# Feature-wise A projections, ScalarE's normalisation and an in-place relu in a two-layer hybrid decoder trunk

## The chip, the cores and the metric

The kernel runs on one core of one Trainium2 chip. Its time is the device time of one execution in microseconds (us). Before the change three runs took 775.15, 771.83 and 767.22 us, a median of 771.83; the profiled execution took 768.9 us.

The core's engines work beside each other, each through its own instructions in order, and wait for each other by semaphores: TensorE (PE, with its weight loads as PEld), VectorE (DVE), ScalarE (ACT), GpSimd (POOL), and SyncE (SP), which issues the DMAs.

## The reference

A trunk of two layers over 512 tokens of width 1024. Each layer normalises the state, multiplies it by one wide matrix `w_in` (its columns belong to four attention branches of four heads each), and brings the gated branches back through `w_out`:

```python
proj = rms_norm(h, norm_pre[layer]) @ w_in[layer]
y_a = mla_branch(a_cq, a_ckv, a_kr, ...) * silu(a_g)      # A: low-rank q and kv, rotary key
y_b = dilated_branch(b_q, b_k, b_v, bias_b) * silu(b_g)   # B
y_c = sparse_branch(c_q, ..., bias_c, k_top) * silu(c_g)  # C: an indexer picks 128 keys
y_d = diff_branch(d_q, d_k, d_v, ...) * silu(d_g)         # D: two softmax maps
h = h + rms_norm(concat(y_a, y_b, y_c, y_d) @ w_out[layer], norm_post[layer])
```

The parts that the change touches:

```python
# A
q = (rms_norm(c_q, q_norm) @ w_uq)       # 192 -> 4 heads x (64 plain + 32 rotary)
kv = (rms_norm(c_kv, kv_norm) @ w_ukv)   # 128 -> 4 heads x (64 key + 64 value)
apply_rope(x) = concat([x1*cos - x2*sin, x1*sin + x2*cos])   # on q's 32 and one shared 32-wide key
p = softmax(mask(q_nope @ k_nope.T + q_rope @ k_rope.T) * 96**-0.5);  o = p @ v
# C's indexer, 8 heads of 32
score = einsum('bqhs,bqh->bqs', relu(q_idx @ k_idx.T), w_idx)   # then mask and top 128
```

## The kernel before, in words

Everything is fp32. Products that need the precision are split into a high and a low part, each in a faster fp32r form, and made of three products (`three`, L1215 to L1217): ScalarE copies the high part (L733 for weights), GpSimd subtracts to get the low part of the weights (`low`, L694), VectorE the low part of activations.

One list, `SEQUENCE`, sets the order of the work; each engine walks through it and issues its share of each step. Steps are: `unit`, one projection of 128 features by 512 tokens or 128 tokens by 256 features (24 matmuls, in one of two PSUM work banks, emptied by ScalarE and VectorE); `idx`, one head of the indexer (three matmuls into three PSUM score banks); `topk`, rounds of VectorE's maximum search; and for each of 16 jobs (a head of D, B, C, A in this order: jobs 0 to 3 are D, 4 to 7 B, 8 to 11 C, 12 to 15 A) `scores`, `norm`, `turn` and `pv`. `layer_steps` lays them out so that while job j makes its scores, job j-1 is normalised and turned and job j-2 or a pair of jobs is multiplied with its values.

For a job with one softmax map: TensorE writes a block of scores; VectorE adds the bias and takes the maximum (L1070, reading PSUM); ScalarE takes the exponential with its sum (L837); VectorE inverts the sums (L981) and scales the four blocks of probabilities, 128, 256, 384 and 512 wide (L984, in `normalise`); TensorE turns them (L1321); ScalarE copies them out of PSUM (L850); TensorE multiplies them with the values (L1349, two jobs at a time). D's jobs have two maps, which VectorE joins (L977).

`TURN_LATE` names the jobs (6, 7, 9, 10, 12) in whose slot the last two turned blocks of the previous job are put off to the next slot, behind the first scores and the `norm` there. Where two jobs are multiplied next, TensorE then waits for just these two copies.

The indexer: ScalarE takes the relu from the score bank into one of four SBUF buffers (L828), VectorE adds the weighted rows into `select` (L1042). TensorE may refill a score bank once the relu is done.

A's projections before are token-wise: per block of 128 tokens (`aup`) one product gives q (L1382, L1383), one k and v (L1386); VectorE scales and rotates q (L1142 to L1151), ScalarE scales k and v (L870 to L874), and `aturn` turns eight 128 x 96 blocks (L1397), which ScalarE copies to `aqk` (L882). They stand in the slots of jobs 10 and 11.

```python
             10: [("aup", 0), ("aup", 1), ("aturn", 0)],
             11: [("aup", 2), ("aturn", 1), ("aup", 3), ("aturn", 2), ("aturn", 3)]}
```

In the slots of jobs 12 to 15 no projections are left beside the attention jobs; from job 16's slot on the output projection begins (`ya`).

## Time and profile before

| | us |
|---|---|
| three runs | 775.15, 771.83, 767.22 |
| profiled execution, whole | 768.9 |
| its span | 767.0 |
| busy in the span: PE / DVE / ACT / POOL | 690.5 / 450.4 / 328.7 / 218.4 |

The profile is of one execution. A busy PE is not a PE at its peak: its matmuls overlap and their ends are modelled, so what a matmul costs is read from the starts of two that follow each other. The granted clock is TensorE's, as a share of 2.4 GHz; 0.50 is its lower level, 1.2 GHz. The chain of waits that the page shows for the end covers only the last 0.2% of the span, so it doesn't help here; the waits of TensorE and its timeline do.

### The profile page before, as it was taken

How to read it: one execution, taken by the hardware profiler on the slowest of the kernel's cores; microseconds unless marked ns; L12 is line 12 of the kernel's file. 1: busy time of each engine (PE TensorE's matmuls, PEld its weight loads, DVE VectorE, ACT ScalarE, POOL GpSimd, SP SyncE). 2: the span in 40 equal slices, each digit the busy share in tenths (PEclk: the TensorE clock that was granted, in tenths of full speed). 3: DMA queues.
4: the chain of work that ended last, by engine and by line, in shares of the span. 5: the costliest groups of instructions: out<-in, count | busy, mean ns of one | idle time of the engine just before them, and what ended most of it. 6: DMA issues, size and time to landing. Idle time of an engine off the chain costs nothing. (4 is left out here: it accounts for less than half of the span.)

```text
span 767.0 us, 10353 instructions
## 1 busy us (share of the span) xinstructions
PE 690.5 (90%) x3836; PEld 553.9 (72%) x3836; DVE 450.4 (59%) x1067; ACT 328.7 (43%) x750; POOL 218.4 (28%) x91
## 2 busy tenths in 40 slices
PE   3996999998989899889998999999898989988996
PEld 2885877787776674448997887788787767444896
DVE  4211597987688645561182158888978864556214
ACT  4422534654223445571434345456432344457221
POOL 1332241424035430200335342324323543020020
PEclk9998999997899976999999999999999997699999
DMA  8457963423122110202353487542322221020112
GB/s 259 123 188 233 258 185 111 124 76 106 55 69 69 69 56 1 109 1 80 96 157 111 129 254 228 157 138 69 98 70 68 70 70 56 0 108 3 43 42 110
DMA packets 66753, 81.47 MB, mean 106 GB/s; under 512 B 10720, under 2 KB 52320, under 8 KB 66703
## 3 DMA queue, kind: packets, MB, share of 16 engines
q1 hardware_dynamic: 66703, 80.81, 34.2%
q8 instruction: 31, 0.51, 0.3%
q14 instruction: 19, 0.16, 0.1%
HBM read 70.28 MB, written 13.93 MB: 110 GB/s over the span
## 5 line engine op out<-in xcount | busy, mean ns | idle before, releaser
L694 POOL TENSOR_TENSOR w_low<-w_raw,w_high 128x2048 fp32r<-128x2048 f32 (+2 forms) x39 | 175.8, 4507 | 435.3 <-ACT w_high L733 435.3
L1215 PE MATMUL bank<-uT,w_high 128*128 128x512 f32 x400 | 161.2, 403 | 0.0
L1217 PE MATMUL bank<-uT,w_low 128*128 128x512 f32 x400 | 159.2, 398 | 0.0
L1216 PE MATMUL bank<-uT,w_high 128*128 128x512 f32 x400 | 159.1, 398 | 0.0
L837 ACT ACTIVATE probs<-probs,negmax 128x128 f32<-128x128 f32 (+3 forms) x160 | 89.1, 560 | 99.6 <-DVE negmax L1070 99.0
L1215 PEld LDWEIGHTS bank<-uT,w_high 128*128 128x128 f32 x400 | 76.2, 190 | 18.7 <-issue 1.9
L1217 PEld LDWEIGHTS bank<-uT,w_low 128*128 128x128 f32 x400 | 76.2, 190 | 18.0
L1216 PEld LDWEIGHTS bank<-uT,w_high 128*128 128x128 f32 x400 | 76.3, 191 | 16.5
L733 ACT ACTIVATE w_high<-w_raw 128x2048 fp32r<-128x2048 f32 (+2 forms) x40 | 74.7, 1868 | 29.8 <-DMA w_raw<-in_w_out 23.7
L1215 PE MATMUL bank<-w_high,mix 128*128 128x256 f32 x256 | 72.4, 283 | 1.0 <-DVE mix L1155 1.0
L1216 PE MATMUL bank<-w_low,mix 128*128 128x256 f32 x256 | 71.6, 280 | 0.0
L1217 PE MATMUL bank<-w_high,mix 128*128 128x256 f32 x256 | 71.6, 280 | 0.0
L1321 PE MATMUL bank<-ident,probs 128*128 128x128 f32 x320 | 52.3, 294 | 20.0 <-DVE probs L984 7.7
L1215 PE MATMUL bank<-w_high,uT 128*128 128x256 f32 (+1 forms) x192 | 55.9, 291 | 12.6 <-ACT values L800 6.0
L1321 PEld LDWEIGHTS bank<-ident,probs 128*128 128x128 f32 x320 | 38.3, 149 | 38.0 <-DVE probs L984 11.9
L850 ACT ACTIVATE turned<-bank 128x512 f32<-128x512 f32 (+3 forms) x128 | 48.5, 430 | 20.3 <-PE bank L1321 19.4
L963 DVE MAX8 best<-select 128x8 f32<-128x512 f32 (+2 forms) x96 | 53.6, 558 | 1.9
L1216 PE MATMUL bank<-w_low,uT 128*128 128x256 f32 (+1 forms) x192 | 54.7, 285 | 0.0
L1217 PE MATMUL bank<-w_high,uT 128*128 128x256 f32 (+1 forms) x192 | 54.6, 284 | 0.0
L964 DVE MATCH_REPLACE8 select<-best,select 128x512 f32<-128x512 f32 (+2 forms) x96 | 52.1, 543 | 0.0
L984 DVE TENSOR_SCALAR probs<-probs,inv 128x128 f32<-128x128 f32 (+1 forms) x96 | 49.7, 581 | 0.8
L1215 PEld LDWEIGHTS bank<-w_high,mix 128*128 128x128 f32 x256 | 48.2, 188 | 1.8 <-DVE mix L1155 1.4
(145 smaller groups left out, 1119.0 us busy)
## 6 DMA issues: line engine op xcount, KB each, us to landing
w_raw<-in_w_in SPq DMA_DIRECT2D x28, 1024.0 KB, 5.4
w_raw<-in_w_out SPq DMA_DIRECT2D x8, 1024.0 KB, 4.9
parts_dram<-staging SPq DMA_DIRECT2D x12, 512.0 KB, 5.9
strips<-strips_dram SPq DMA_DIRECT2D x24, 256.0 KB, 4.6
dqk<-parts_dram SPq DMA_DIRECT2D x24, 256.0 KB, 4.3
hX<-in_x SPq DMA_DIRECT2D x8, 512.0 KB, 5.8
strips_dram<-table_dram SPq DMA_DIRECT2D x1, 3328.0 KB
qidx<-parts_dram SPq DMA_DIRECT2D x12, 256.0 KB, 4.2
```

What stands on the lines that cost most here:

```text
L694: nc.gpsimd.tensor_tensor(w_low[:, s, :, 0:w], w_raw[:, s, :, 0:w], w_high[:, s, :, 0:w].bitcast(F32), ALU.subtract).then_inc(w_low_done, 1)
L733: nc.scalar.activation(w_high[:, g % SLOTS, :, 0:w], w_raw[:, g % SLOTS, :, 0:w], ACT.Copy).then_inc(w_high_done, 1)
L837: nc.scalar.activation(pr, pr, ACT.Exp, bias=negmax[:, j % 4, m, q:q + 1], scale=-1.0, accum_out=sums[:, j % 4, m, q:q + 1]).then_inc(exp_ ...
L850: nc.scalar.activation(turned[j % 2][:, TOFF[kb]:TOFF[kb] + w], bank[:, TURN + t % 2, 0:w], ACT.Copy).then_inc(turn_emptied, 1)
L963: after(nc.vector.max(best[:], row))
L964: after(nc.vector.match_replace(row, best[:], row, MARK))
L984: ins = nc.vector.tensor_scalar(probs[bufs[0]][:, sl], probs[bufs[0]][:, sl], inv[:, i, 0, q:q + 1], None, ALU.mult)
L1215: nc.tensor.matmul(out_ap, lh, rh, start=start, stop=False)
L1216: nc.tensor.matmul(out_ap, lh, rl, start=False, stop=False)
L1217: return nc.tensor.matmul(out_ap, ll, rh, start=False, stop=stop)
L1321: ins = nc.tensor.transpose(bank[:, TURN + t % 2, (q - kb) * P:(q - kb + 1) * P], buf[:, POFF[q] + kb * P:POFF[q] + (kb + 1) * P], ident[:])
```

## The change

Three edits.

**The indexer's relu.** ScalarE writes it back into the score bank, and VectorE's weighted sum reads it there. TensorE may refill the bank only once that sum is done.

**The normalisation.** For jobs of B, C and A (4 to 15) VectorE only inverts the sums; ScalarE scales the four blocks, in place, at the same step of the list. D's jobs stay as they are.

**A's projections.** They are made feature-wise: `aq` per head (128 features, the 32 rotary ones twice, the second time with their halves swapped, by 512 tokens), `ak` for two heads of keys, `av` for two blocks of values. There is no scaling by token at the copies: k's root is brought into `latkv` by one product of the roots with the identity and one VectorE multiply (`aroot`), q's root goes in as the scale of A's bias step. q's rotation is one multiply with a table (`trig`), since the score product over 128 rows adds the two halves. The shared key is rotated by GpSimd and copied to all heads by DMA. The eight turned blocks fall away. The q weights come in six DMAs for two and k and v's in two for one, and six small DMAs per layer are new for the tables and the rotary key.

```diff
-             10: [("aup", 0), ("aup", 1), ("aturn", 0)],
-             11: [("aup", 2), ("aturn", 1), ("aup", 3), ("aturn", 2), ("aturn", 3)]}
+             10: [("aq", 0), ("aq", 1), ("aroot",), ("aq", 2)],
+             11: [("aq", 3), ("ak", 0), ("ak", 1), ("av", 0), ("av", 1)]}
...
# SyncE
                 if step == ("norm", 3):
-                    sp.dma_start(wuq[:, 0, :], mla_w_uq[l, 0:P, :]).then_inc(a_loaded, 16)
...
+                    sp.wait_ge(scores_ready, l * NS + NS_IDX)
+                    sp.dma_start(trig[HD:P, :], rope).then_inc(trig_loaded, 16)
+                if step == ("norm", 8):
+
+                    sp.wait_ge(bias_ready, (l + 1) * HEADS)
+                    wait_unit_emptied(sp, l * NU + UNIT_AT[("unit", "cq", 1)])
+                    sp.dma_start(trig2[HD:A_QK, :], rope[A_ROPE:2 * A_ROPE, :]).then_inc(krx_loaded, 16)
+                    sp.dma_start(krx[HD:HD + 16, :], latq[HD + 16:A_QK, 1, :]).then_inc(krx_loaded, 16)
+                    sp.dma_start(krx[HD + 16:A_QK, :], latq[HD:HD + 16, 1, :]).then_inc(krx_loaded, 16)
+                if step == ("norm", 9):
+
+                    sp.wait_ge(kr_ready, l + 1)
+                    sp.wait_ge(scores_ready, l * NS + NS_IDX + S_AT[8])
+                    for first in (HD, A_QK):
+                        sp.dma_start(aqk[first:first + A_ROPE, 1, :, :],
+                                     latq[HD:A_QK, 1, :].unsqueeze(1).to_broadcast([A_ROPE, HEADS, SEQ])
+                                     ).then_inc(krope_loaded, 16)
...
# GpSimd
+                if step == ("norm", 8):
+
+                    pool.wait_ge(trig_loaded, 16 * (l + 1))
+                    pool.wait_ge(krx_loaded, 48 * (l + 1))
...
+                    nc.gpsimd.tensor_tensor(raw, raw, trig[HD:A_QK, :], ALU.mult).then_inc(kr_step, 1)
+                    pool.wait_ge(kr_step, 2 * l + 1)
+                    nc.gpsimd.tensor_tensor(turn, turn, trig2[HD:A_QK, :], ALU.mult).then_inc(kr_step, 1)
+                    pool.wait_ge(kr_step, 2 * (l + 1))
+                    nc.gpsimd.tensor_tensor(raw, raw, turn, ALU.add).then_inc(kr_ready, 1)
...
# ScalarE
                         act.wait_ge(scores_ready, n + 1)
-                        if relus[0] >= 4:
-                            act.wait_ge(index_added, relus[0] - 3)
-                        nc.scalar.activation(probs[relus[0] % 4][:, 0:WID[q]],
-                                             bank[:, SCORE + n % 3, 0:WID[q]], ACT.Relu).then_inc(relu_done, 1)
-                        relus[0] += 1
+                        b = bank[:, SCORE + n % 3, 0:WID[q]]
+                        nc.scalar.activation(b, b, ACT.Relu).then_inc(relu_done, 1)
...
+                if kind == "norm" and MAPS[step[1]] == 1:
+                    j = step[1]
+                    buf = probs[probs_buffers(j)[0]]
+                    act.wait_ge(inv_ready, scaled(l, j))
+                    for q in range(NB):
+                        pr = buf[:, POFF[q]:POFF[q] + WID[q]]
+                        ins = nc.scalar.activation(pr, pr, ACT.Copy, scale=inv[:, j % 4, 0, q:q + 1])
+                    ins.then_inc(probs_scaled, 1)
...
+                if kind == "aq":
+                    n = l * NU + UNIT_AT[step]
+                    act.wait_ge(unit_ready, n + 1)
+                    nc.scalar.activation(aqk[0:HD, 0, step[1], :], bank[0:HD, unit_bank(n), :], ACT.Copy
+                                         ).then_inc(high_written, 1)
...
# VectorE
-                    after(nc.vector.reciprocal(inv[:, i, 0], sums[:, i, 0]))
-                    for q in range(NB):
-                        sl = slice(POFF[q], POFF[q] + WID[q])
-                        ins = nc.vector.tensor_scalar(probs[bufs[0]][:, sl], probs[bufs[0]][:, sl],
-                                                      inv[:, i, 0, q:q + 1], None, ALU.mult)
-                ins.then_inc(probs_ready, 1)
+                    nc.vector.reciprocal(inv[:, i, 0], sums[:, i, 0]).then_inc(inv_ready, 1)
...
-                        nc.vector.scalar_tensor_tensor(row, probs[relus[0] % 4][:, 0:WID[q]], wi[:, q, h:h + 1],
+                        n = l * NS + h * 3 + SEL_BLOCKS.index(q)
+                        nc.vector.scalar_tensor_tensor(row, bank[:, SCORE + n % 3, 0:WID[q]], wi[:, q, h:h + 1],
                                                        before, ALU.mult, ALU.add).then_inc(index_added, 1)
...
+                        scale = negroot[:, q:q + 1] if br == "A" else -1.0
...
+                if kind == "aq":
...
+                    nc.vector.tensor_tensor(aqk[HD:P, 0, step[1], :], bank[HD:P, unit_bank(n), :], trig[HD:P, :],
+                                            ALU.mult).then_inc(emptied_by["dve"], 1)
...
# TensorE
                     if ii < NS_IDX:
-                        pe.wait_ge(relu_done, ll * NS_IDX + ii + 1)
+                        pe.wait_ge(index_added, ll * NS_IDX + ii + 1)
...
+                    nc.tensor.matmul(b, wuq[:, 0, h, :], latq[:, 0, :], start=True, stop=False)
+                    nc.tensor.matmul(b, wuq[0:QL - P, 1, h, :], latq[0:QL - P, 1, :], start=False, stop=True
+                                     ).then_inc(unit_ready, 1)
...
+                        ins = nc.tensor.matmul(b[:, tb * P:(tb + 1) * P],
+                                               roots[:, r, NB + tb:NB + tb + 1].to_broadcast([P, P]), ident[:],
+                                               start=True, stop=True)
...
+                    nc.tensor.matmul(b, wukv[:, 0, step[1] * P:(step[1] + 1) * P], latkv[:], start=True, stop=True
+                                     ).then_inc(unit_ready, 1)
...
+                        ins = nc.tensor.matmul(b[:, half * 256:(half + 1) * 256], latkv[:, tb * P:(tb + 1) * P],
+                                               wukv[:, 1, :], start=True, stop=True)
```

How the order moves, at three places of the first layer. The names in the rows: `values_61` holds the values of the branch at work, `probs_55` to `probs_58` are the four probability buffers, `turned_59` and `turned_60` the two for turned blocks, `bank` is PSUM.

ScalarE at the third block of B's values (slot of job 6), before:

```order
L837 ACTIVATE probs_57,sums<-probs_57,negmax 128x128 [waits shifted]
L837 ACTIVATE probs_57,sums<-probs_57,negmax 128x256 [waits shifted]
L800 ACTIVATE values_61<-bank 128x256 [waits unit_ready,pv_ready] x3
L733 ACTIVATE w_high<-w_raw 128x8x256 [waits w_loaded0]
L850 ACTIVATE turned_60<-bank 128x512 [waits turn_ready,pv_ready]
```

and with the change:

```order
L874 ACTIVATE probs_57,sums<-probs_57,negmax 128x128 [waits shifted]
L874 ACTIVATE probs_57,sums<-probs_57,negmax 128x256 [waits shifted]
L882 ACTIVATE probs_56<-probs_56,inv 128x128 [waits inv_ready]
L882 ACTIVATE probs_56<-probs_56,inv 128x256
L882 ACTIVATE probs_56<-probs_56,inv 128x384
L882 ACTIVATE probs_56<-probs_56,inv 128x512
L840 ACTIVATE values_61<-bank 128x256 [waits unit_ready,pv_ready] x3
L773 ACTIVATE w_high<-w_raw 128x8x256 [waits w_loaded0]
```

The four scalings of job 5 stand between the exponentials of job 6 and the copies of B's values.

TensorE in the slot of job 10, before (the first rows of A's projections, then the turn of job 9):

```order
L1382 MATMUL bank<-wuq,latq 128x384 [waits emptied_by_dve,a_folded]
L1383 MATMUL bank<-wuq,latq 128x384
L1386 MATMUL bank<-wukv,latkv 128x512 [waits emptied_by_dve]
L1382 MATMUL bank<-wuq,latq 128x384 [waits emptied_by_dve,a_folded]
L1383 MATMUL bank<-wuq,latq 128x384
L1386 MATMUL bank<-wukv,latkv 128x512 [waits emptied_by_act]
L1321 MATMUL bank<-ident,probs_56 128x128 [waits turn_emptied,probs_ready]
L1321 MATMUL bank<-ident,probs_56 128x128 x3
```

and with the change:

```order
L1405 MATMUL bank<-latq,wuq 128x512 [waits emptied_by_dve,a_folded]
L1406 MATMUL bank<-latq,wuq 128x512
L1405 MATMUL bank<-latq,wuq 128x512 [waits emptied_by_dve,a_folded]
L1406 MATMUL bank<-latq,wuq 128x512
L1351 MATMUL bank<-ident,probs_56 128x128 [waits turn_emptied,probs_scaled]
L1351 MATMUL bank<-ident,probs_56 128x128 x3
```

Four products of 512 columns stand where two groups of 384, 384 and 512 columns stood; `ak` and `av` come in the next slot, and the products with `tokq` and `tokk` are gone.

ScalarE in the slot of job 13, before:

```order
L850 ACTIVATE turned_60<-bank 128x512 [waits turn_ready,pv_ready]
L850 ACTIVATE turned_60<-bank 128x384 [waits turn_ready]
L837 ACTIVATE probs_56,sums<-probs_56,negmax 128x128 [waits shifted]
L837 ACTIVATE probs_56,sums<-probs_56,negmax 128x256 [waits shifted]
L850 ACTIVATE turned_60<-bank 128x256 [waits turn_ready]
L850 ACTIVATE turned_60<-bank 128x128 [waits turn_ready]
L837 ACTIVATE probs_56,sums<-probs_56,negmax 128x384 [waits shifted]
L837 ACTIVATE probs_56,sums<-probs_56,negmax 128x512 [waits shifted]
```

and with the change:

```order
L895 ACTIVATE turned_60<-bank 128x512 [waits turn_ready,pv_ready]
L895 ACTIVATE turned_60<-bank 128x384 [waits turn_ready]
L874 ACTIVATE probs_56,sums<-probs_56,negmax 128x128 [waits shifted]
L874 ACTIVATE probs_56,sums<-probs_56,negmax 128x256 [waits shifted]
L882 ACTIVATE probs_55<-probs_55,inv 128x128 [waits inv_ready]
L882 ACTIVATE probs_55<-probs_55,inv 128x256
L882 ACTIVATE probs_55<-probs_55,inv 128x384
L882 ACTIVATE probs_55<-probs_55,inv 128x512
L895 ACTIVATE turned_60<-bank 128x256 [waits turn_ready]
L895 ACTIVATE turned_60<-bank 128x128 [waits turn_ready]
L874 ACTIVATE probs_56,sums<-probs_56,negmax 128x384 [waits shifted]
L874 ACTIVATE probs_56,sums<-probs_56,negmax 128x512 [waits shifted]
```

The scaling of job 12 stands ahead of the last two copies of job 11's turned blocks, on which the product of jobs 10 and 11 waits.

## Rows read from the trace of the kernel before

**Rows 1.** The page, its first part: busy us, share of the span, instructions

```profile
PE 690.5 (90%) x3836; PEld 553.9 (72%) x3836; DVE 450.4 (59%) x1067; ACT 328.7 (43%) x750; POOL 218.4 (28%) x91
```

**Rows 2.** Waits of TensorE: in total, times, longest us

```profile
PE bank L1321 <- DVE probs L984: 7.7, 6, 2.8
```

**Rows 3.** Windows, columns: length, PE, PEld, DVE, ACT, POOL, clock, DMA share, GB/s

```profile
184.00:197.00 13.00, 13.00 (x47) 10.82 (x46) 8.72 (x24) 3.91 (x8) 4.54 (x1) 0.50 0.08 22
223.00:231.00 8.00, 5.00 (x40) 4.65 (x39) 7.59 (x28) 2.90 (x8) 1.60 (x1) 1.00 0.00 0
264.00:273.00 9.00, 9.00 (x38) 5.22 (x38) 4.57 (x14) 5.38 (x15) 2.92 (x3) 0.62 0.01 3
283.00:299.00 16.00, 16.00 (x41) 9.15 (x41) 9.93 (x32) 4.01 (x14) 4.61 (x2) 0.50 0.01 2
321.00:347.00 26.00, 21.35 (x114) 12.36 (x115) 18.66 (x64) 18.60 (x55) 0.00 (x0) 1.00 0.14 52
552.00:562.00 10.00, 8.62 (x56) 7.32 (x57) 8.72 (x21) 4.79 (x10) 2.49 (x2) 1.00 0.09 28
...
629.00:637.00 8.00, 8.00 (x32) 4.61 (x32) 4.38 (x14) 5.38 (x15) 2.92 (x3) 0.62 0.01 3
```

**Rows 4.** TensorE by time near job 7's wait: start, us, what, idle

```profile
263.95 0.98 PE L1321 MATMUL bank<-ident,probs 128*128 128x128 f32 x7 [2.80 <-DVE probs L984]
...
273.11 0.50 PE L1215 MATMUL bank<-uT,w_high 128*128 128x512 f32 x1
```

**Rows 5.** VectorE's normalisation at the same place, and at its shortest

```profile
256.74 7.16 DVE L984 TENSOR_SCALAR probs<-probs,inv 128x128 f32<-128x128 f32 x4
...
322.91 1.27 DVE L984 TENSOR_SCALAR probs<-probs,inv 128x128 f32<-128x128 f32 x4
```

**Rows 6.** GpSimd by time at the same place

```profile
258.68 4.60 POOL L694 TENSOR_TENSOR w_low<-w_raw,w_high 128x2048 fp32r<-128x2048 f32 x1
```

**Rows 7.** Groups of instructions on ScalarE: busy us, mean ns of one, idle before

```profile
L837 ACT ACTIVATE probs<-probs,negmax 128x128 f32<-128x128 f32 (+3 forms) x160 | 89.1, 560 | 99.6 <-DVE negmax L1070 99.0
...
L870 ACT ACTIVATE tokk<-bank,roots 128x256 f32<-128x256 f32 x8 | 3.8, 476 | 24.1 <-PE bank L1386 24.1
```

**Rows 8.** VectorE's groups by form: the weighted sum, a reader of PSUM

```profile
L1042 DVE SCALAR_TENSOR_TENSOR select<-probs,wi,select 128x512 f32<-128x512 f32 x14 | 26.2, 1875 | 12.1 <-ACT probs L828 12.1
...
L1070 DVE CUSTOM_DVE_ANT_0 probs<-bank,strips 128x512 f32<-128x512 f32 x24 | 16.5, 689 | 1.0 <-PE bank L1298 0.6 <-PE bank L1217 0.2
```

**Rows 9.** TensorE by time at the indexer's last head

```profile
100.34 0.51 PE L1279 MATMUL bank<-kidx,qidx 96*128 96x512 f32 x1 [0.71 <-ACT probs L828]
```

**Rows 10.** TensorE and ScalarE by time at the third block of B's values

```profile
226.48 0.36 PE L1215 MATMUL bank<-w_high,uT 128*128 128x256 f32 x1 [3.00 <-ACT values L800]
225.97 0.63 ACT L800 ACTIVATE values<-bank 128x256 f32<-128x256 f32 x2
```

**Rows 11.** TensorE, ScalarE at the products of jobs 4, 5 and 8, 9

```profile
243.75 2.37 PE L1349 MATMUL bank<-turned,values 128*64 128x512 f32 x16 [1.71 <-ACT turned L850]
305.28 2.38 PE L1349 MATMUL bank<-turned,values 128*64 128x512 f32 x16 [1.54 <-ACT turned L850]
304.70 0.53 ACT L850 ACTIVATE turned<-bank 128x256 f32<-128x256 f32 x2
```

**Rows 12.** TensorE by time in A's projections

```profile
307.58 0.91 PE L1382 MATMUL bank<-wuq,latq 128*128 128x384 f32 x2
...
309.26 1.12 PE L1386 MATMUL bank<-wukv,latkv 128*128 128x512 f32 x2
310.23 0.60 PE L1397 MATMUL bank<-ident,tokq 128*96 128x128 f32 x4
...
319.26 0.61 PE L1397 MATMUL bank<-ident,tokq 128*96 128x128 f32 x4 [1.20 <-ACT aqk L882]
```

**Rows 13.** TensorE by time: first score of A, first turn of its last head

```profile
321.04 2.58 PE L1301 MATMUL bank<-aqk 96*128 96x128 f32 x8 [0.36 <-ACT aqk L882]
347.32 0.93 PE L1321 MATMUL bank<-ident,probs 128*128 128x128 f32 x7
```

211 lines of the change are left out of this document (97 added, 114 removed).

## The prediction

> **What bounds the kernel now.** I read the page's busy times first: TensorE is busy 90% of the span, VectorE much less [rows 1]. So work taken off VectorE pays only where TensorE waits for it. Next the waits of TensorE: the reader is to see that L984, the normalisation, is in them with 7.7 us, 2.8 the longest [rows 2]. Third the windows: in them the reader is to see that TensorE's clock falls to its lower level, 1.2 GHz, in the same places of both layers: after job 7's wait, and after the one-column products ahead of A's projections [rows 3]. A fall costs half of its length. The places are where the change acts, so I go through one layer by place; the second repeats it nearly to the microsecond. About 1% (7.7 us) is what this kernel's measurement can tell from no change. The sum is made against the profiled execution, 768.9 us; the median of the three runs, 771.8, lies 2.9 above it.
>
> **The normalisation's price.** On VectorE four scalings take 1.27 us undisturbed and 7.16 at job 7, where GpSimd's additions and a 4.60 us `w_low` run beside them [rows 5, 6]. On ScalarE the row does not exist. Above it lies the exponential over the same four widths, mean 560 ns, so 2.24 us for four; below, VectorE's 1.27. A scaling by a pointer, 256 wide, takes 476 ns [rows 7] against the exponential's 560 at mean 320. Back-to-back instructions overlap by about 0.1 us. I take 1.85 us, 24 times in the run, 44 us of ScalarE's time.
>
> **Job 7 (gain).** TensorE waits 2.80 us for L984, then runs turns, C's scores and the product of jobs 6 and 7 until 273.11 [rows 4]; the window from 264 to 273 has a mean clock of 0.62, in layer two 629 to 637 likewise [rows 3]. From the end of the wait's unit at 261.15 (263.95 less 2.80) that is 11.96 us. With ScalarE doing it, GpSimd does not matter and the scaling is done 2 us before TensorE wants it: the wait goes, and some 7.4 us at half clock become 3.7. Late next are the copies of job 7's last two turned blocks, behind job 8's exponentials: about 1.1 us. Net -5.4 us.
>
> **B's values, job 6 (loss).** TensorE waits 3.00 us for ScalarE's first copy of B's values, which starts at 225.97 right behind job 6's first two exponentials [rows 10]. In the changed order job 5's four scalings stand between. The wait grows by 1.85 to 4.85. The cause of the first 3.00, VectorE's late scores, stays.
>
> **Products of jobs 4, 5 and 8, 9 (loss).** Both wait for the last two copies of turned blocks, 1.71 and 1.54 us [rows 11], and both times a scaling now stands ahead of these copies: +1.85 and +1.8.
>
> **A's projections (gain).** One token block costs TensorE 1.68 us for q (307.58 to 309.26) and 0.97 for k and v; four turned blocks have records of 0.60 that overlap [rows 12], and I take 0.48. Before: four times 2.65, eight times 0.48, and 0.5 for the rotary key, 14.9 us. After, at the row's price of 0.97 for 512 fp32 columns: eight products for q 7.8, `ak` 1.9, `av` 2.0 (four of 256), `aroot` 1.1 (four of 128), 12.8. That is -2.1 at full clock. About 5.6 us of the old work stands in the 283 to 299 window at 0.50 [rows 3] and 3.9 of the new, which saves 1.7 more; `aroot` gives back 0.5: -1.2. The waits for tokk, tokq and aqk go, the largest 1.20 [rows 12], 2.3 in all. New are two small waits, for the last of the q banks and at A's first score: +0.6. Net -5.0 us.
> I cost the rotary key at nothing. Its chain is a load, three GpSimd additions over 512, each a quarter of a `w_low`'s 4.60 [rows 6], so 3.5 us, and a copy to all heads. It can start when the last `fill` is done, soon after job 7's turn at 263.95, and must end by A's first score at 321.04 [rows 4, 13]: even with 10 us for each of two DMA steps it ends 30 us early. Without that cover it would cost its length, up to 24. The six DMAs more in SyncE's queue hold nothing up: the weight load behind them waits for the gate's unit anyway.
>
> **A's jobs (loss).** From 321 to 347 no projection covers TensorE. ScalarE is busy 18.6 of 26 us there [rows 3]; five normalisations (jobs 11 to 15) add 9.25, which makes 27.9. So ScalarE now sets the pace. Walking its order from A's first score at 321.04 to the first turn of job 15, at 347.32 before [rows 13], which leaves 1.4 us of ScalarE waiting for scores, I get 29.3 us for 26.3: +3.0 (ends: 1.6, the pure fill, and 9.25, if every scaling lands on the path; the order has other work of TensorE beside most).
>
> **The indexer.** VectorE's weighted sum over 512 has a mean of 1.88 us, disturbed by GpSimd; a reader of PSUM of this width takes 0.69 undisturbed [rows 8]. That frees some 8 us of VectorE per layer, which nobody on the path waits for: VectorE catches up with TensorE in the stretch of D's jobs anyway. But a score bank is free only after relu and sum. Behind the first heads a projection stands between and hides this; the last two heads stand together, where TensorE waits 0.71 now [rows 9], and each bank comes up to 0.69 later, the sum's own length [rows 8]: +0.6 (ends: -1.2 if the end of the contention counts most, +3 if each head loses 0.4).
> The Trainium skill ("ScalarE: Activation LUTs", section "Step-by-step: what each stage is for") says that ScalarE writes PSUM faster than SBUF, which would make the in-place relu cheaper than before. No row here shows such a write. By that rule the three relus of a head would end sooner, and the term would be nearer 0, the sum 1 us lower.
>
> **The sum.** Per layer: job 7 -5.4, B's values +1.85, jobs 4 and 5 +1.85, jobs 8 and 9 +1.8, A's projections -5.0, A's jobs +3.0, the indexer +0.6: -1.3, or -2.6 for two.
> The clock is left. A wait does not make it fall for certain: the same stretch of the program has 0.50 in layer one (184 to 197) and 1.00 in layer two (552 to 562) [rows 3]. Three waits of 3.4 to 4.9 us are new or longer, and one of 2.8 is gone. I take one fall more than before in one of the layers, +3.7 by job 7's price. 768.9 - 2.6 + 3.7 = 770; against the median **773 us**.
>
> **The rivals.**
> *Forecast, the stalls trade (0.38):* 773, own range 765 to 781.
> *Slower, the clock falls at the new waits (0.31).* Place: B's values (4.85 us), the products of jobs 4, 5 (3.56) and 8, 9 (3.35). For it: the 2.80 wait does it in both layers. Against it: the 3.00 wait does not (223 to 231 at 1.00), nor do A's waits (321 to 347) [rows 3]. Price 3.7 each; after jobs 8, 9 come A's fp32 products, which stayed at 0.50 for the 16 us of 283 to 299, so up to 8 there. It decides from two falls on: 773 + 7.4 = 780; all of them in both layers would give 800. Its middle is 787. The Trainium skill ("TensorE: Matmul & The Clock Gate", section "HAM oscillation — how this bites in real kernels") describes the mechanism, a wait that makes the engine start again at the low clock.
> *Faster, ScalarE's scalings don't reach TensorE (0.27).* If the reciprocal comes early enough for ScalarE to scale in its idle time before the exponentials' wait ends, and VectorE's free time brings scores forward, then the 1.85 + 1.85 + 1.8 vanish and A's jobs lose 1 instead of 3: -1.3 - 7.5 = -8.8 per layer, with no fall more: 771.8 - 17.6 = 754. For it: ScalarE is busy only 43% of the span. Against it: the order puts the scalings behind exponentials that are themselves late.
> *The indexer doesn't gain and the bank wait bites (0.04).* Were TensorE to wait 1.3 us (a relu and a sum) at each of seven handovers of heads, that is +9 per layer: 790.
>
> Range 757 to 790. Faster by over 1%: 0.28; within: 0.38; slower: 0.34.
>
> **What would show it.** L984 gone, a ScalarE scaling of four blocks at 1.7 to 2.0 us; no wait at job 7 and clock 1.00 behind it; the wait at the third block of B's values at 4.9; the waits of the two products at 3.5; 29 us from A's first score to job 15's turn with ScalarE busy 27; the weighted sum at 0.7 for 512; A's q product at 0.97 per 512 columns. Wrong would be: the window behind 4.9 us of waiting at 0.50, B's wait still at 3.0, or a wait of A's first score for the rotary key's DMA.

## The result, and the profile after

The changed kernel takes 795.98 us (median of 4 runs, 789.99 to 801.93) where the kernel before takes 772.5 (4 runs): a ratio of 1.029, 95% interval 1.018 to 1.040. A second timing on another chip gave 1.030 (1.024 to 1.035). It is 3% slower, where the forecast was 773 in a range of 757 to 790. Each kernel's executions fall into a faster and a slower group, and a ratio is that of the faster ones, so it need not be that of the two medians. The profiled execution took 789.99 us with a span of 788.2 and a mean clock of 0.932; before, 768.9, 767.0 and 0.954.

The page after: busy times as in [rows 1], and the clock in 40 slices.

```profile
PE 699.4 (89%) x3788; PEld 560.5 (71%) x3788; DVE 378.4 (48%) x931; ACT 364.8 (46%) x826; POOL 225.6 (29%) x97
...
PEclk9998999999989968999999999999798997689998
```

VectorE is 72 us less busy, ScalarE 36 more, as the change says. TensorE has 48 instructions fewer and is busy 8.9 us longer, and its idle time (span less busy) went from 76.5 to 88.8 us. So there are two losses to find: waits, and work that ran slower.

Waits of TensorE after (in total, times, longest us), the lines that answer to [rows 2, 10, 11]:

```profile
PE bank L1379 <- ACT turned L895: 20.4, 8, 4.5
...
PE bank L1240 <- ACT values L840: 9.6, 2, 4.8
PE bank L1351 <- ACT probs L882: 7.8, 6, 1.7
...
PE bank L1304 <- DVE select L1076: 3.6, 4, 1.6
...
PE bank L1405 <- DVE wukv L1154: 1.5, 1, 1.5
```

TensorE by time in layer one: the third block of B's values, the products of jobs 4, 5 and 8, 9, job 7's first turn, the first and a later product of A's q, a late one at full clock, A's first score, a turn, and job 15's first turn.

```profile
222.70 0.55 PE L1240 MATMUL bank<-w_high,uT 128*128 128x256 f32 x1 [4.80 <-ACT values L840]
...
243.68 4.07 PE L1379 MATMUL bank<-turned,values 128*64 128x512 f32 x16 [3.52 <-ACT turned L895]
...
262.62 0.93 PE L1351 MATMUL bank<-ident,probs 128*128 128x128 f32 x7
...
284.06 2.07 PE L1405 MATMUL bank<-latq,wuq 128*128 128x512 f32 x2 [1.48 <-DVE wukv L1154]
...
288.07 2.07 PE L1405 MATMUL bank<-latq,wuq 128*128 128x512 f32 x2
...
305.44 4.03 PE L1379 MATMUL bank<-turned,values 128*64 128x512 f32 x16 [4.51 <-ACT turned L895]
309.40 1.12 PE L1405 MATMUL bank<-latq,wuq 128*128 128x512 f32 x2
...
318.46 1.47 PE L1328 MATMUL bank<-aqk 128*128 128x128 f32 x6
...
323.34 0.98 PE L1351 MATMUL bank<-ident,probs 128*128 128x128 f32 x7 [1.72 <-ACT probs L882]
...
350.09 0.98 PE L1351 MATMUL bank<-ident,probs 128*128 128x128 f32 x7 [0.64 <-ACT probs L882]
```

Every wait that was forecast is there, at its length: 4.80 for 4.85, 3.52 for 3.56, job 7's gone. Only that of jobs 8, 9 is longer, 4.51 for 3.35. Both products take 4.03 to 4.07 us where they took 2.37 [rows 11], and a q product takes 2.07 at 288 and 1.12 at 309. This is the lower level of the clock. The windows after, columns as in [rows 3], say the same:

```profile
219.00:227.00 8.00, 4.30 (x20) 4.33 (x21) 5.93 (x22) 3.33 (x10) 0.02 (x1) 0.57 0.00 0
243.00:248.00 5.00, 4.32 (x17) 1.88 (x18) 0.21 (x1) 0.62 (x3) 0.68 (x1) 0.66 0.00 0
263.00:270.00 7.00, 6.29 (x39) 4.00 (x38) 3.28 (x11) 6.25 (x18) 4.83 (x4) 1.00 0.05 13
281.00:299.00 18.00, 16.52 (x40) 8.34 (x39) 7.29 (x20) 6.99 (x18) 2.91 (x2) 0.53 0.08 17
305.00:310.00 5.00, 4.56 (x18) 1.82 (x18) 0.48 (x1) 2.19 (x3) 2.73 (x1) 0.66 0.00 0
...
602.00:610.00 8.00, 6.39 (x32) 6.25 (x33) 3.90 (x13) 2.57 (x7) 0.00 (x0) 0.57 0.00 0
625.00:630.00 5.00, 4.78 (x20) 2.54 (x21) 0.69 (x1) 0.17 (x2) 0.21 (x1) 0.66 0.00 0
...
687.00:692.00 5.00, 4.63 (x18) 1.93 (x18) 0.51 (x1) 2.12 (x3) 2.80 (x1) 0.66 0.00 0
```

Behind each of the three waits, in both layers, the clock is low; behind job 7 (263 to 270) it is at its full level, which it was not before [rows 3]. I also added up, over windows of 1 us from the span's start to its end, what each lacks to a clock of 1.00: 35.6 us before, 53.7 after. Below this sum is called the clock's loss. It is an upper bound of what the clock costs, since some of it lies in TensorE's waits; within TensorE's busy time it is 33.5 us before and 46.8 after.

Why the waits are there is read on ScalarE by time, ahead of the product of jobs 4 and 5:

```profile
240.80 0.49 ACT L874 ACTIVATE probs<-probs,negmax 128x256 f32<-128x256 f32 x1
241.20 0.19 ACT L874 ACTIVATION_READ_ACCUMULATOR probs<-probs,negmax 128x1 f32 x1
241.29 1.90 ACT L882 ACTIVATE probs<-probs,inv 128x128 f32<-128x128 f32 x4
243.10 0.52 ACT L895 ACTIVATE turned<-bank 128x256 f32<-128x256 f32 x2
```

Job 6's scaling, 1.90 us long and not wanted until later, stands ahead of the copy that TensorE waits for.

### The profile page after: what moved, and what is told of

Its sections match the earlier page's. It is cut to its first block and busy times, and to the rows that moved or that the text cites. A ratio compares the mean times of both kernels' runs of the same rounds, so it can differ in the third digit from the quotient of the medians.

```text
span 788.2 us, 10171 instructions
## 1 busy us (share of the span) xinstructions
PE 699.4 (89%) x3788; PEld 560.5 (71%) x3788; DVE 378.4 (48%) x931; ACT 364.8 (46%) x826; POOL 225.6 (29%) x97
## 5 line engine op out<-in xcount | busy, mean ns | idle before, releaser
L1240 PEld LDWEIGHTS bank<-uT,w_high 128*128 128x128 f32 x400 | 77.1, 193 | 19.0 <-issue 2.0
L1241 PEld LDWEIGHTS bank<-uT,w_high 128*128 128x128 f32 x400 | 77.3, 193 | 16.7
L1240 PE MATMUL bank<-w_high,uT 128*128 128x256 f32 (+1 forms) x192 | 58.5, 305 | 15.5 <-ACT values L840 9.6
L1241 PE MATMUL bank<-w_low,uT 128*128 128x256 f32 (+1 forms) x192 | 57.0, 297 | 0.0
L1242 PE MATMUL bank<-w_high,uT 128*128 128x256 f32 (+1 forms) x192 | 57.0, 297 | 0.0
L1379 PE MATMUL bank<-turned,values 128*64 128x512 f32 (+3 forms) x192 | 34.7, 513 | 20.4 <-ACT turned L895 20.4
L1240 PEld LDWEIGHTS bank<-w_high,uT 128*128 128x128 f32 x192 | 39.3, 205 | 17.1 <-issue 14.9
```

The source lines that it names most:

```text
L1240: nc.tensor.matmul(out_ap, lh, rh, start=start, stop=False)
L1241: nc.tensor.matmul(out_ap, lh, rl, start=False, stop=False)
L1242: return nc.tensor.matmul(out_ap, ll, rh, start=False, stop=stop)
L1379: ins = nc.tensor.matmul(bank[HD * half:HD * (half + 1), PV, kb * P:SEQ], v[:, kb, hs], tr[:, TOFF[kb]:TOFF[kb] + P * (NB - kb)], start=kb ...
```

## The experiments

Times are compared with the kernel before, run on the same chip; the ratio is given with its 95% interval. Each of these groups shared a chip: e1, e2, e3, e5; e4, e6, e7, e8; e9, e10, e11, e13; e12, e14, e15, e16.

**Undo the scaling: e1_norm_back.** The changed kernel, with VectorE scaling again.

```diff
-                    nc.vector.reciprocal(inv[:, i, 0], sums[:, i, 0]).then_inc(inv_ready, 1)
+                    after(nc.vector.reciprocal(inv[:, i, 0], sums[:, i, 0]))
+                    for q in range(NB):
+                        ...
+                        ins = nc.vector.tensor_scalar(probs[bufs[0]][:, sl], probs[bufs[0]][:, sl],
+                                                      inv[:, i, 0, q:q + 1], None, ALU.mult)
...
```

> The change with only its normalisation undone: VectorE scales the probabilities of B, C and A again; A's projections and the in-place relu stay. Theory 1 (the loss is ScalarE's scaling, which stands ahead of copies that TensorE waits for, and the clock falls that these waits bring): TensorE's waits of 4.80, 3.52 and 4.51 us go back to about 3.0, 1.7 and 1.5, job 7's wait of 2.8 comes back, and the run takes 758 to 768, some 28 to 38 us less than the change. Theory 2 (the loss is in A's feature-wise projections or in the relu): it stays above 785.

762.41 us, 0.982 (0.972 to 0.992). Its waits of TensorE:

```profile
PE bank L1376 <- ACT turned L887: 8.9, 4, 2.7
...
PE bank L1237 <- ACT values L840: 6.0, 2, 3.0
```

TensorE waits 3.0 for B's values and 2.71 at jobs 8, 9, not the 1.5 expected there. The scaling on ScalarE is the whole loss, and more: without it the change gains 1.8%.

**The scaling alone: e2_norm_only.** The kernel before, and in it the change's ScalarE step and waits for it:

```diff
+                if kind == "norm" and MAPS[step[1]] == 1:
+                    ...
+                    act.wait_ge(inv_ready, scaled(l, j))
+                    for q in range(NB):
+                        pr = buf[:, POFF[q]:POFF[q] + WID[q]]
+                        ins = nc.scalar.activation(pr, pr, ACT.Copy, scale=inv[:, j % 4, 0, q:q + 1])
+                    ins.then_inc(probs_scaled, 1)
```

> The kernel before with only the normalisation moved to ScalarE. Theory 1: the waits at the third block of B's values, and at the products of jobs 4, 5 and 8, 9 grow to 4.8, 3.5 and 3.4 or more as in the change, the clock falls behind them, and the run takes 795 to 808, slower than the change since A's gain is missing. Theory 2: within 1% of before, 765 to 780.

790.56 us, 1.020 (1.013 to 1.027), a loss as expected, but a smaller one than the 795 to 808 said, and than the change's own. The waits are 4.80, 3.5 and 3.34; the last is what the prediction said for jobs 8, 9. The further 1.17 of the change come with the new projections: ScalarE's copy (0.59 us) and behind it VectorE's multiply (0.69) empty a q bank, and job 10's first maxima and exponentials, behind which job 9's last copies stand, come only then. TensorE's idle time is 92.8 us, 16.3 more than before, and the clock's loss 36.8, 1.2 more: here the loss is almost all waiting.

**A's projections alone: e3_a_only.** e1_norm_back with the old relu too, so that of the change only the new projections are left:

```diff
-                        b = bank[:, SCORE + n % 3, 0:WID[q]]
-                        nc.scalar.activation(b, b, ACT.Relu).then_inc(relu_done, 1)
+                        if arelus[0] >= 4:
+                            act.wait_ge(index_added, arelus[0] - 3)
+                        nc.scalar.activation(probs[arelus[0] % 4][:, 0:WID[q]],
+                                             bank[:, SCORE + n % 3, 0:WID[q]], ACT.Relu).then_inc(relu_done, 1)
...
```

> The kernel before with only A's feature-wise projections (normalisation on VectorE, relu into SBUF). Theory 1: the 5 us per layer that I gave to this part are there, 760 to 768. Theory 2: slower than before by 10 or more.

768.12 us, 0.986 (0.980 to 0.991): a gain of 11 us by the ratio.

**The relu alone: e4_idx_only.** The kernel before, and in it:

```diff
-                        if relus[0] >= 4:
-                            act.wait_ge(index_added, relus[0] - 3)
-                        nc.scalar.activation(probs[relus[0] % 4][:, 0:WID[q]],
-                                             bank[:, SCORE + n % 3, 0:WID[q]], ACT.Relu).then_inc(relu_done, 1)
+                        b = bank[:, SCORE + n % 3, 0:WID[q]]
+                        nc.scalar.activation(b, b, ACT.Relu).then_inc(relu_done, 1)
...
```

> The kernel before with the in-place relu alone. By the prediction's working it gives time back to VectorE that nobody on the path waits for, and costs at most a bank wait at the last two heads: within 0.5% of before (768 to 776 against 772), TensorE's waits in the indexer 2 us per layer as before. Rival: VectorE's freed 8 us per layer bring the waits for its scores forward, and the time falls by 1% or more. Other rival: the bank wait grows to 1.3 us at each handover of heads, and it is 1% slower or more.

769.57 us against 769.5, 1.002 (0.997 to 1.007): nothing that can be measured, as expected. TensorE's waits for the relu's reader are 3.6 us for the whole run, where its waits for the relu were 4.2 in six before, and VectorE's weighted sum is down to a mean of 748 ns (512 wide) from [rows 8]'s 1875:

```profile
PE bank L1277 <- DVE select L1040: 3.6, 4, 1.6
...
L1040 DVE SCALAR_TENSOR_TENSOR select<-bank,wi,select 128x512 f32<-128x512 f32 x14 | 10.5, 748 | 18.9 <-ACT bank L827 18.9
```

Two things lie behind these means. The old 1875 is a mean of two kinds: ten of the fourteen sums took 740 to 745 ns, and four, with GpSimd at work beside them, 4.70 us. And the longest of the waits grew from 1.1 to 1.60 us. In the 13 traces with the in-place relu the clock falls behind that wait for 3.4 us (1.7 lost) in 22 of 26 layers; at the same place of the five with the old relu in none of ten. The time shows nothing of it, since other falls come and go too: the clock's loss of e4_idx_only is 33.3 us for 35.6 before.

**The same scalings, behind the copies: e5_behind.** In ScalarE's order alone, six scalings of a layer (jobs 5, 6, 7, 9, 10, 12) are put behind the copies that TensorE waits for; the work is the same.

```diff
+        if step[0] == "norm" and MAPS[step[1]] == 1:
+            j = step[1]
+            stop = [("turn", j - 1, NB - 1)] if seq[i + 1][1] == ("turn", j - 1, 2) else \
+                [("unit", "bv", 1)] if j == 5 else None
+            if stop:
+                k = next(k for k in range(i, len(seq)) if seq[k][1] == stop[0])
+                seq[i:k] = seq[i + 1:k + 1]
+                seq[k] = (l, step)
```

> The change with ScalarE's four scalings put off in ScalarE's own order: behind the last two copies of the previous job's turned blocks where these stand in the same slot (jobs 7, 8, 10, 11 and 13), and behind the first two copies of B's values in the slot of job 6. No work is added or left out. Theory 1, order: the waits of 4.80, 3.52 and 4.51 us fall by 1.85 each and the falls of the clock at B's values and at jobs 4, 5 go, 775 to 783. If the place in the queue does not matter and only ScalarE's load does: no change, 790 to 802.

763.42 us, 0.986 (0.978 to 0.995), better than the 775 to 783 expected. ScalarE by time, ahead of the same product (246.68 here for 243.10 above): the copy now stands ahead of the scaling.

```profile
246.58 0.19 ACT L893 ACTIVATION_READ_ACCUMULATOR probs<-probs,negmax 128x1 f32 x1
246.68 0.52 ACT L914 ACTIVATE turned<-bank 128x256 f32<-128x256 f32 x2
247.10 1.91 ACT L901 ACTIVATE probs<-probs,inv 128x128 f32<-128x128 f32 x4
```

Its busy times and waits of TensorE:

```profile
PE 688.7 (90%) x3788; PEld 552.7 (72%) x3788; DVE 378.7 (49%) x931; ACT 363.6 (47%) x826; POOL 225.7 (29%) x97
...
PE bank L1398 <- ACT turned L914: 10.3, 6, 2.7
PE bank L1370 <- ACT probs L901: 7.8, 6, 1.7
```

The order alone is worth 4.3% of before, 33 us. These waits themselves are only 13.7 of them (20.4 to 10.3, and 9.6 to 6.0 for B's values). The rest I put down to the clock, by subtraction. The two profiles bear out a part: their spans differ by 21.8 us, 11.1 of idle and 10.7 of busy time, and the clock's loss is 41.8 here for 53.7. The profiled execution was the slowest of the four of e5_behind and the fastest of the four of the change, so the pair shows less than the medians.

**Is it idleness that lowers the clock? e6_fill.** The changed kernel with its order; TensorE transposes a constant while it would wait.

```diff
+            def fill_bank(n):
+                for _ in range(n):
+                    nc.tensor.matmul(bank[:, PV, 0:P], ident[:], ident[:], start=True, stop=True)
...
-                    pe.wait_ge(turn_emptied, (l * NJ + PV_JOBS[i][-1] + 1) * NB)
                     if l * NPV + i > 0:
                         pe.wait_ge(pv_emptied, l * NPV + i)
+                    fill_bank({5: 14, 9: 18}.get(PV_JOBS[i][-1], 0))
+                    pe.wait_ge(turn_emptied, (l * NJ + PV_JOBS[i][-1] + 1) * NB)
...
+                    if step == ("unit", "bv", 2):
+                        pe.wait_ge(pv_emptied, l * NPV + HEADS)
+                        fill_bank(19)
```

> The changed kernel, and in it TensorE transposes a constant into a free bank, 128 columns of fp32 at a time, while it would wait: 19 times before the third block of B's values, 14 times before the product of jobs 4 and 5, 18 times before that of jobs 8 and 9, at about 0.24 us each. No useful work is added or taken away, and each wait's end stays where it was. If idle time is what makes the clock fall there, the falls right behind these three places (3.4, 1.7 and 1.7 us lost per layer) vanish, and the run is 10 to 14 us faster than the changed kernel, 782 to 786 on its chip. If the clock falls for another reason (the fp32 product behind the waits, say), the falls stay and the time is that of the changed kernel or a little longer.

779.52 us against 769.5, 1.009 (1.004 to 1.014): from 1.029, 15 us gained by work that serves nothing, for the 10 to 14 expected. Its busy times, the filling, and the windows behind the three places:

```profile
PE 703.8 (91%) x3992; PEld 572.5 (74%) x3992; DVE 378.6 (49%) x931; ACT 364.2 (47%) x826; POOL 225.3 (29%) x97
...
L1262 PE MATMUL bank<-ident 128*128 128x128 f32 x204 | 23.8, 275 | 0.0
```

```profile
216.00:224.00 8.00, 7.53 (x66) 7.34 (x65) 7.55 (x27) 3.33 (x10) 1.65 (x1) 1.00 0.00 0
239.00:244.00 5.00, 4.61 (x35) 3.13 (x34) 0.40 (x1) 2.13 (x6) 2.20 (x3) 1.00 0.00 0
301.00:306.00 5.00, 4.61 (x21) 1.85 (x22) 0.69 (x1) 2.23 (x4) 2.78 (x1) 1.00 0.00 0
```

All three falls are gone, in layer two as well. TensorE is busy 703.8 us here, 23.8 of it filling, so 680.0 with the work that took 699.4; idle and filling together are 90.2, as the 88.8 of the changed kernel. So the waits stood as they were, and the work ran 19.4 us faster in this execution; the timing has 15. The clock's loss is 31.3 us, 22.4 less than in the changed kernel: 13.7 of them stood behind the three places, 5.1 in A's jobs, whose own waits are unchanged and whose falls are gone too, and the rest lies at A's projections and elsewhere. So a fall here also bears on what comes after it.

**Which jobs should ScalarE scale? e7_hybrid and e8_job7.** As e5_behind, but ScalarE scales jobs 4 to 10 only, or job 7 only, and VectorE the others.

```diff
+ON_ACT = [4, 5, 6, 7, 8, 9, 10]     (e8_job7: [7])
...
-        if step[0] == "norm" and MAPS[step[1]] == 1:
+        if step[0] == "norm" and step[1] in ON_ACT:
...
```

> The changed kernel with ScalarE's scalings of jobs 4 to 10 behind the copies that TensorE waits for, and the scalings of A's jobs 11 to 15 on VectorE again. If A's jobs lost time because ScalarE was full there, TensorE's 7.8 us of waiting for A's probabilities shrinks to about 5 and the run is 3 to 8 us faster than the one with all scalings behind (763 on a chip where before took 775): 755 to 760. If it was not ScalarE's fill, no change: 760 to 766.

> The changed kernel with ScalarE scaling job 7 alone (the one where VectorE's scaling takes 7.16 us beside GpSimd) and VectorE all the others. If job 7 is the only place where the moved scaling pays, as the prediction has it (5.4 us per layer), this is the best of all: the wait of 2.8 us at job 7 and the clock's fall behind it go, and the products of the pairs wait 1.7 us or less; 752 to 758 where before takes 773 to 775. If the fall has another cause than job 7's wait, it is that of the version with all scalings on VectorE: 762.

763.86 us, 0.989 (0.982 to 0.996), and 763.29, 0.988 (0.980 to 0.996): both no better than e1_norm_back, and e8_job7 not in the 752 to 758 expected. In e8_job7 job 7's wait is gone in both layers and TensorE's idle time is 72.9 us for e1_norm_back's 76.3, but it is busy 685.2 for 679.3, and the clock's loss is 36.2 for 30.6. At A's first q products in layer one it is 8.5 for 3.4 us. Behind job 3's turn it is 5.1 and 6.8 us in the two layers, where e1_norm_back has none; falls there come and go between traces of kernels whose wait there is the same. TensorE now comes to A's first q product before VectorE has folded `wukv`, waits, and stays at the low clock that the one-column products ahead of it left:

```profile
281.75 2.07 PE L1433 MATMUL bank<-latq,wuq 128*128 128x512 f32 x2 [1.62 <-DVE wukv L1181]
...
285.75 2.07 PE L1433 MATMUL bank<-latq,wuq 128*128 128x512 f32 x2
```

In e1_norm_back there is no such wait, and the clock is back with the next record:

```profile
286.51 1.83 PE L1402 MATMUL bank<-latq,wuq 128*128 128x512 f32 x2
288.27 1.12 PE L1403 MATMUL bank<-latq,wuq 64*128 64x512 f32 x2
```

e8_job7 starts its first q product 4.8 us ahead of e1_norm_back and its third 1.1 us behind it (295.84 and 294.77).

**Place by place: e9_again, e11_bv, e10_p89, e12_p45.** The changed kernel once more, and with one of the moved scalings of e5_behind alone (the edit is shown against e5_behind):

```diff
-            if stop:
+            if stop and j in (5,):     (e10_p89: (10,), e12_p45: (6,))
```

> The changed kernel once more, unchanged, as the measure for the three beside it. Its first timing had a ratio of 1.029 with an interval of 1.018 to 1.040. If the loss is the program's own, the ratio lies in that interval again and TensorE waits 4.80, 3.52 and 4.51 us at the three places. If the clock's falls at a place are chance, the profile shows them at other places than the first, at a like total of 40 to 55 us lost to the clock.

> The changed kernel with one scaling moved in ScalarE's order: job 5's, behind the first two copies of B's values. If each place's wait and its clock's fall are a price of their own: the wait goes from 4.80 to 3.00 us in each layer (3.6 in all) and the fall behind it (3.4 each) with it, 4 to 10 us faster than the changed kernel. Rival: the falls have one budget over the span, so that one place undone brings them back at another, and only the 3.6 us of the wait are gained.

> The changed kernel with one scaling moved in ScalarE's order: job 10's, behind the last two turned copies of job 9. The wait before the product of jobs 8 and 9 goes from 4.51 to 2.71 us in each layer (3.6 in all). The fall behind it (1.7 each) may go too: 4 to 7 us faster than the changed kernel. The sum over the three places would be 16 to 24 us of the 32 that all moves together gave; if it comes out smaller, the places aren't independent.

> The changed kernel with one scaling moved in ScalarE's order: job 6's, behind the last two turned copies of job 5. The wait before the product of jobs 4 and 5 goes from 3.52 to 1.7 us in each layer (3.6 in all) and the fall behind it (1.7 each) may go. The other two places gave 11.6 and 9.7 us, all three together 33. If the places are independent, this one gives 10 to 12 us; if the three together gave more than the sum of each, 5 to 7.

| kernel | us | ratio, 95% | clock's loss |
|---|---|---|---|
| e9_again | 796.42 | 1.030 (1.024 to 1.035) | 60.3 |
| e11_bv, B's values | 782.18 | 1.015 (1.008 to 1.022) | 44.8 |
| e10_p89, jobs 8, 9 | 785.23 | 1.017 (1.011 to 1.023) | 53.7 |
| e12_p45, jobs 4, 5 | 793.86 | 1.026 (1.018 to 1.034) | 65.5 |

The last three each have one wait less by 1.8 us a layer, 3.6 in all. B's values give 12 us, jobs 8, 9 10 us, jobs 4, 5 3 us (within the error of nothing); together 24 of 33. None of the three hit what was expected of it (4 to 10, 4 to 7, and 10 to 12 or 5 to 7). The other three moves of e5_behind (jobs 7, 9, 12) were not run alone; that of job 12 takes away two waits of 1.27 and 1.62 us at the product of jobs 10, 11. In the profile of e12_p45 the fall behind the product of jobs 4, 5 is gone and another stands earlier (185 to 200, 6.8 us lost), one that the kernel before shows too, at 184 to 197 [rows 3], and e9_again not. So the falls are not a price that each place has for itself.

**The scaling alone, in the good order: e14_norm_behind.** e2_norm_only with e5_behind's order.

> The kernel before (A's projections and the relu as they were) with the scaling on ScalarE, each scaling behind the copies that TensorE waits for. With the scalings in the program's order the same kernel was 2.0% slower than before. If the order alone made that loss and the gain at job 7 (5.4 us per layer in the prediction) is real, it is now 1% faster than before, 763 to 768. If the gain at job 7 is eaten by ScalarE's fill in A's jobs, it is within 0.5% of before, 771 to 777.

773.73 us, 1.003 (0.999 to 1.007), from 1.020. With these waits at their old lengths the scaling costs nothing measurable; neither does it gain. Job 7's wait of 2.8 is gone in both layers, but TensorE waits for scaled probabilities as long as before in all, 7.6 us for 7.7, now in A's jobs (1.70, 1.46 and 0.62 in layer one). Job 7's gain is not to be seen here, nor between e1_norm_back (0.982) and e5_behind (0.986).

**Keep TensorE busy: e13_warm, e15_warm_dve, e16_before_warm.** Filling as in e6_fill, but at more places: before job 3's turn, the third block of B's values, the products of jobs 4, 5 and 8, 9, job 7's turn (where VectorE scales it) and A's first q product (in the new projections), and one transpose behind the one-column products of each of the first three blocks. It stands on e8_job7, on e1_norm_back, and on the kernel before.

```diff
+                    if step == ("turn", 3, 0):
+                        pe.wait_ge(turn_emptied, jj * NB - 1)
+                        fill_bank(8, TURN + jj * NB % 2)
...
+                    if h == 0:
+                        fill_bank(6, unit_bank(n))
                     pe.wait_ge(a_folded, l + 1)
...
+                            fill_bank(1, unit_bank(n))
```

> A candidate to beat both: ScalarE scales job 7 alone, and TensorE transposes a constant while it waits (128 columns of fp32 each): 8 times before job 3's turn, 12 before the third block of B's values, 6 before the product of jobs 4 and 5, 10 before that of jobs 8 and 9, 6 before A's first q product, and once behind each block's one-column products. If the clock's falls stand behind idle time, the 37 us that this arrangement lost to the clock without the filling shrink to 20 or less, and the ratio to before comes to 0.96 to 0.975. If the falls behind the one-column products are not of idle time, their 8.5 and 3.4 us stay and the ratio is 0.98. If the filling delays useful work, it is above 0.988, the value without it.

> All scalings on VectorE, A's new projections and the in-place relu as in the change, and TensorE filled with transposes of a constant at every wait of over 1 us in the middle of the layer: job 3's turn (8), the third block of B's values (12), the product of jobs 4 and 5 (6), job 7's turn (11), the product of jobs 8 and 9 (10), A's first q product (6), one behind each block's one-column products. The same filling with job 7 scaled by ScalarE gave a ratio of 0.9745. If what job 7's wait cost was the clock, this gives the same, 0.970 to 0.978. If the wait itself is worth what it lasts, it is 4 us slower, 0.98.

> The kernel before, with the same filling at its own waits (job 3's turn 8, B's values 12, the product of jobs 4 and 5 6, job 7's turn 11, the product of jobs 8 and 9 6, one-column products 1 a block), and none of the change. Its clock cost 37 us in the profile, some 20 of them behind these places. If keeping the clock is a gain by itself, the ratio is 0.975 to 0.985. If the filled version's gain came from A's projections and job 7 alone, it is 0.995 to 1.00.

| kernel | us | ratio, 95% | clock's loss | without filling |
|---|---|---|---|---|
| e13_warm | 754.16 | 0.975 (0.970 to 0.979) | 27.2 | 0.988 |
| e15_warm_dve | 756.44 | 0.981 (0.975 to 0.987) | 21.9 | 0.982 |
| e16_before_warm | 761.65 | 0.987 (0.980 to 0.994) | 27.3 | 1 |

e13_warm is the fastest version, 20 us below before and 42 below the change. Filling alone makes the kernel before 1.3% faster. With all scalings on VectorE it gave nothing measurable (0.981 for 0.982), although the clock's loss fell from 30.6 to 21.9; why is open. The two kernels were timed on two chips, with intervals of 0.6 and 1% to each side, so a gain of under 1% could hide. Beside it, ScalarE's scaling of job 7 would be worth 0.65% (e13_warm to e15_warm_dve), but these too were on two chips and the two intervals overlap, so this is not shown. e13_warm hit its ratio but not its loss of 20 us or less; e16_before_warm lies between its two expectations, so keeping the clock is a gain by itself, and a smaller one than said.

## Why the prediction was wrong

**The mechanism was in it, as the slower rival, at 0.31.** That rival named the three places and said 780 to 800; the time was 796. The step that failed is the clock's term, "I take one fall more than before in one of the layers, +3.7". There were six new ones at the three places, one at each in each layer, with 13.7 us of the clock's loss, and seven more elsewhere with 15.4: three in A's jobs, two behind the relu's wait, two at D's scores and turn in layer two. Job 7's two and one ahead of B's values were gone. e6_fill prices the low clock behind the three places, and what hangs on it, at 15 us of the run.

The Trainium skill ("TensorE: Matmul & The Clock Gate", section "HAM oscillation — how this bites in real kernels") has this mechanism, an engine that starts again at the low clock after a wait, and the windows agree: 0.57 and 0.66 behind the waits, 1.00 in the same places once they were filled.

The step rested on a comparison: B's old wait of 3.00 us had no fall behind it in this trace [rows 3], so 4.85 was taken as likely to have none. Over the 15 traces without complete filling (the kernel before, after, and all but e13_warm, e15_warm_dve and e16_before_warm) I counted the falls that start in a wait or at most 2.5 us behind it; all of these waits began at the full clock. Of the 18 waits of 3.00 for B's values 7 had a fall behind them, so the row of one trace was one draw of a thing that goes either way. Of the 30 waits of 3.3 us and longer at the three places, all 30 had one. A wait at job 7 of 2.8 had one in 7 of 8, the product's wait of 2.71 in 2 of 12, and these two began within 0.6 us of the end of another fall.

**The sum, part by part.** The two profiles split the time as the prediction did, if the clock is counted within TensorE's busy time alone:

| us, both layers | forecast | measured |
|---|---|---|
| TensorE's waits | +11.4 | +12.3 |
| its work at the full clock | -4.2 | -4.4 |
| the clock | -6.1 | +13.3 |
| the span | +1.1 | +21.2 |

The forecast's clock is job 7's -3.7 and the projections' -1.2 in each layer, and +3.7 for the one fall. So nearly the whole miss is the clock. That the waits agree so well is in part luck, as the places below show.

**B's values, jobs 4, 5: right.** 4.80 and 3.52 for 4.85 and 3.56. **Jobs 8, 9: the growth right, the base wrong.** The growth was 1.8 (2.71 to 4.51); the base rose from 1.54 to 2.71 with the new projections, which the prediction didn't follow through ScalarE's and VectorE's order. That is 2.3 us over two layers.

**The price of a scaling: right.** 1.90 us in the row above for the 1.85 taken.

**Job 7: mechanism right, size wrong.** The wait and the fall behind it are gone (263 to 270 at 1.00), and "late next", costed at 1.1 us, is a wait of 0.71 at the product of jobs 6 and 7. Of the 5.4 us per layer nothing measurable arrived in the three comparisons without filling (e5_behind, e8_job7, e14_norm_behind). e8_job7 shows where it went: 3.4 us of idle time less, 5.9 of busy time more, with the low clock at A's q products of layer one and behind job 3's turn. The prediction looked no further than the next copies.

**A's projections: the sum right, with luck.** -5.0 per layer was said, -10 in all; e3_a_only measured a ratio of 0.986, 11 us. But its idle time is 76.7 us, as before (76.5), where -3.4 was said: the old waits are gone, and others, that at jobs 8, 9 above all, grew as much. Busy time fell by 10.0 us for the 6.6 said, since the low clock at the q products lasted 6.8 us for 17.1 before. In the changed kernel TensorE comes there earlier; the wait for `wukv` (1.48 in layer one) was not foreseen, and 281 to 299 has 0.53. The rotary key cost nothing, as said: A's first score (318.46) has no wait.

**A's jobs: nearly right.** From A's first score to job 15's first turn 31.6 us (318.46 to 350.09) for the 29.3 forecast; one fall (1.7 us lost at 339 to 343) is in it. Giving A's scalings back to VectorE (e7_hybrid against e5_behind, 0.989 and 0.986, on two chips) gained nothing that the timing shows, so these 3 us were also no loss that decides.

**The indexer: right in the whole, not in its parts.** Nothing measurable in the whole (e4_idx_only); the waits got 0.6 us shorter, not 1.2 longer, and falls of the clock came behind the longest, which was not foreseen. The Trainium skill ("ScalarE: Activation LUTs", section "Step-by-step: what each stage is for") has ScalarE's writes to PSUM faster than those to SBUF, and would have had the term nearer 0. The traces agree in the small: the relus took 588, 458 and 367 ns in place of 595, 493 and 392 (512, 384 and 256 wide). The measurement can't tell the two terms: it was 1.2 us over two layers, the interval of e4_idx_only 4 to each side.

**The forecast's own balance.** By its terms all but the one fall came to -2.6 us. The runs give: projections -11, relu 0, scaling in the good order +2 or +3. What is left of the 24 us of loss is the order: 33 us, 14 of waiting and, by subtraction, 19 of clock, of which e6_fill measures 15. That the order could be put right at no cost was not considered; ScalarE's scalings could go behind those copies without TensorE waiting for them longer (7.8 us in e5_behind as in the change).

The other rival, "scalings don't reach TensorE", failed by what was said against it: the scaling stands behind the next job's exponentials, and these are late. In the rows of ScalarE above, it starts at once when they end, at 241.29, and nothing of it lies in idle time.

What stays open: why the wrong order costs 1.7% on the old projections (e2_norm_only to e14_norm_behind) and 4.3% on the new (after to e5_behind). The waits shrink about alike, TensorE's idle time by 13.5 us on the old and 11.1 on the new. The clock's loss is 36.8 and 35.1 us on the old, though e2_norm_only has a fall at each of the three places as well, and 53.7 and 41.8 on the new. The low clock at the projections lasts 10.2 us per layer in e2_norm_only and e14_norm_behind, 17.1 and 20.5 in the change, 20.5 and 6.8 in e5_behind; this points to the q products, whole products of 512 columns, but it was not isolated. Open is as well what decides whether a wait of 2 to 3 us has a fall behind it. Open, too, is e15_warm_dve's missing gain.

## What to carry to other kernels

Before work is moved to an engine that is idle half of the time, walk that engine's own queue at each handover: the moved piece must stand behind whatever the busy engine is waiting for, and here this alone decided between 1.4% faster and 3% slower (e5_behind and the change). Price a wait of the bounding engine with the clock that follows it, and where one trace shows no fall behind a wait, look at other layers and runs before taking that as a rule. If such a wait can't be removed, useless work on the waiting engine may cost less than its idleness.

## What the runs showed of the hardware

- Useless work can shorten a run: 51 transposes per layer (204 records in both, 23.8 us busy, 0.23 a transpose) in place of idle time took 15 us off it.
- With the clock low, a further wait went with a low clock behind it. A's first q product comes behind the one-column products. Over 11 kernels with the new projections (after and e1, e3, e5 to e12), 22 layers: where that product waited 1.3 to 1.6 us for `wukv` (11 times), the products behind it all ran at 1.2 GHz (2.07 us a record pair); where it didn't, 8 of 11 were back at 2.4 GHz (1.12 or 1.13) by the third. No run changed this wait alone.
- TensorE can arrive earlier and be later: e8_job7 was 4.8 us ahead of e1_norm_back at A's first q product and 1.1 us behind at its third.
- VectorE's weighted sum, 512 wide, takes 740 to 745 ns from SBUF with GpSimd idle and 4.70 us with GpSimd at work (four of 14, kernel before). From PSUM it took 740 to 752 ns, with GpSimd at work too.
